# A hybrid decoder layer on one core: the second pair of x tiles is loaded behind the modulation weights

## The chip, the core and the metric

The kernel runs on one core of one Trainium2 chip. Its engines are TensorE (PE, with PEld for the loading of its stationary operand), VectorE (DVE), ScalarE (ACT), GpSimd (POOL) and SyncE (SP). SP and POOL issue the DMA transfers of this kernel, each from a queue of its own: q1 is that of SP, q0 that of POOL. The metric is the time of one execution on the device, in microseconds (us), as the median of several.

## What is computed

One decoder layer with two kinds of heads side by side. Only its beginning matters here:

```python
shift, scale, gate = split(c @ w_ada + b_ada, 3)     # c: (1, 1024), w_ada: (1024, 3072)
h = rms_norm(x, norm_g) * (1 + scale) + shift        # x: (2048, 1024)
u = h @ w_in                                         # all inputs of the heads, gates among them
# mLSTM heads and forgetting attention on u, then
x = x + gate * (concat(heads) @ w_out)
```

So nothing can be projected before `shift` and `scale` are known, and they need two thirds of `w_ada` (8 MB) and the whole of `c`.

## The kernel before

The sequence has 2048 tokens, in four blocks `b` of 512; the model width of 1024 is cut into eight slices `k` of 128. All engines run instruction streams of their own that are written out by hand and meet at semaphores; there is no scheduler. What follows is the first stage (`modulate_and_project`), up to about 98 us of the profile.

**Loads.** x comes in pairs of tiles of 128 tokens, 1 MB each, into a ring of four buffers: pairs 0 and 1 in `u_copy`, pair 2 in `work`, pair 3 in `stage[:, 1]`. `load_x(i)` (L246) issues one. The modulation weights come in five pieces (`PIECES`, `load_piece`, L242) of 2, 2, 2, 1 and 1 rows of 128 x 2048 numbers, a MB each row, into `ada_rows`. SP issues in this order: c, pair 0, pair 1, the five pieces, pair 2, a weight tile of `w_in`, pair 3, the gates' columns, another weight tile (L252 to L262). Pairs 4 to 7 are issued as the ring comes free, pairs 4 and 5 when the eight slices of block 0 have been transposed (L265). Beside it POOL issues 13 small parameter loads (L334 to L347), which all count up `param_landed`.

**Modulation.** PE transposes c and the parameters (L754, L756; the second waits for all 13 loads). DVE copies both out, and then adds up the eight rows of `w_ada`, each times its column of c, into `ada_sum` (L478, L481), each as its piece lands. 16 products of one column (L810, counted as 32 in the trace) sum that over the partitions into `ps_mod`, and three short DVE instructions make `scale`, `shift` and `gain` (L488 to L492), of which `mod_ready` tells.

**x.** For each pair i ACT takes squares and a root (`root_mean_square(i)`, L869 and L872), DVE takes the reciprocal (`inverse(i)`, L449), and ACT multiplies the two tiles by it (`scale_x(i)`, L893); for pairs 4 to 7 DVE does the multiplication (`normalize`, L456).

**The steps.** There are 32 steps, at = 8 b + k. In each, PE transposes slice k of the four tiles of block b into PSUM (`turn_x`, L771, four transposes), ACT modulates it (`modulate`, L880), and DVE splits the result in a high and a low part (`split_h`, L464 and L466). PE then multiplies them with the first weight tile and the gates' columns (`first_products`, L783, three products; `gate_products`, L797, two). The products of a step stand in PE's stream behind the turn of four steps later (`LAG`). For block 0 there is room in PSUM for five turns (`ps_first`), and they are issued first of all, ahead of L810. `turn_x(b, 0)` waits until all four tiles of its block are scaled; `turn_x` of b > 0 also until ACT has taken the slice two steps before; `modulate` also until DVE has split the slice two steps before.

After the stage the projections of the other tiles follow on PE (L703), which need every block of h, and everything later stands behind them.

Of the kernel before, what the change touches and what calls it, by code (L numbers as in the profile page):

```python
# [71 lines left out]
def modulate_and_project(nc, block, a, scratch, keep, fox):  # L72

    with ExitStack() as ctx:
# [19 lines left out]
        with ExitStack() as late:  # L94
# [142 lines left out]
            def _(sp):  # L237
# [15 lines left out]
                load_x(0)  # L253
                load_x(1)
                for q in range(len(PIECES)):
                    load_piece(q)
                load_x(2)
                load_w(0, F_Q)
# [170 lines left out]
            def _(dve):  # L429
# [41 lines left out]
                inverse(0)  # L471
                inverse(1)
                dve.wait_ge(c_ready, 1)
                for q, (first, end) in enumerate(PIECES):
                    dve.wait_ge(piece_landed[q], 16)
                    for k in range(first, end):
                        if k == 0:
                            dve.tensor_scalar(ada_sum, ada_rows[k], c_cols[:, k:k + 1], None, ALU.mult).then_inc(ada_added, 1)  # L478
                        else:
                            dve.wait_ge(ada_added, k)  # L480
                            dve.scalar_tensor_tensor(out=ada_sum, in0=ada_rows[k], scalar=c_cols[:, k:k + 1], in1=ada_sum,  # L481
                                                     op0=ALU.mult, op1=ALU.add).then_inc(ada_added, 1)
                split_w(0, 1, 0)
                dve.wait_ge(half_free, 1)
                inverse(2)
                inverse(3)
                dve.wait_ge(mod_psum, 1)
# [5 lines left out]
                                         in1=params[:, ADA_ROWS + 2 * KT:ADA_ROWS + 3 * KT],  # L493
                                         op0=ALU.add, op1=ALU.mult).then_inc(mod_ready, 1)

                def split_gates():
# [11 lines left out]
                for b in range(TB):  # L508
                    for k in range(KT):
                        split_h(b, k)  # L510
                        if (b, k) == (0, 0):
                            split_gates()
                        if 0 < b < TB - 1 and k in (2, 5):
                            normalize((b + 1) * G_PAIRS + (k == 5))
                    if b == 1:
                        split_w(1, 1, 1)
# [173 lines left out]
            def _(pe):  # L690
# [112 lines left out]
                ahead = len(ps_first)  # L803
                for k in range(ahead):
                    turn_x(0, k)
                pe.wait_ge(zeroed, 5)
                pe.wait_ge(ada_added, KT)
                for col in range(2 * KT):
                    first = (D_MODEL + col * P) % (2 * D_MODEL)
                    ins = pe.matmul(ps_mod[:, col:col + 1], ada_sum[:, first:first + P], one[:, :], start=True, stop=True)  # L810
                ins.then_inc(mod_psum, 1)
                done = 0
                for at in range(ahead, TB * KT + LAG):
# [39 lines left out]
            def _(act):  # L853
# [40 lines left out]

                for i in range(ON_ACT * G_PAIRS):
                    root_mean_square(i)
                    if i == 1:
                        scale_x(0)
                        scale_x(1)
                scale_x(2)  # L900
                act.wait_ge(mod_ready, 3)
                for b in range(TB):
                    for k in range(KT):
                        modulate(b, k)
                        if b == 0 and k in (1, 3):
                            scale_x(3, [k // 2])
                        if 0 < b < TB - 1 and k in (1, 4):
                            root_mean_square((b + 1) * G_PAIRS + (k == 4))
                        if b and k == 5:
                            take_gates(b - 1)  # L910
# [1276 lines left out]
```

## Time and profile before

| | us |
|---|---|
| median of 3 runs | 1593.19 |
| lowest and highest | 1592.62, 1593.48 |
| span of the profiled execution | 1588.24 |
| start of the first product of a step (L783) in it | 43.72 |
| start of the turn that opens block 1 (L771) | 50.52 |
| start of the squares of pair 4 (L869) | 54.33 |
| start of the projections behind the stage (L703) | 97.94 |

The span counts from the first to the last recorded work of the core. The profiled execution's time by the clock of the runs is not recorded; the span is 4.95 us less than the median, and this is taken as what lies around it. In the profile's page the chain of waits is followed back from the last instruction: at each step to what released it. PE is busy for 95% of the span.

### The profile page before, as it was taken

The page shows a single profiled execution, that of the slowest core. Times are in us where ns is not written, and L with a number is a line of the kernel's source. Part 1 is how long each engine was busy: PE and PEld are TensorE (multiplying, and loading weights), DVE is VectorE, ACT ScalarE, POOL GpSimd, SP SyncE. Part 2 cuts the span into 40 slices and gives each one's busy share as a digit, 9 for nine tenths or more (in the row PEclk, how much of TensorE's full clock was granted, in tenths as well). Part 3 has the DMA queues.
Part 4 walks back from the last instruction along what each step waited for, and adds up shares of the span by engine and source line. Part 5 has one row for each costly group of instructions (what it writes and reads, how often), then busy time and mean ns, then how long its engine had stood idle before and what let it go on. Part 6 is the DMA issues. An engine that isn't in the chain of part 4 may idle for free.

```text
span 1588.2 us, 21410 instructions
## 1 busy us (share of the span) xinstructions
PE 1515.7 (95%) x7913; PEld 1152.1 (73%) x7913; DVE 792.8 (50%) x1835; ACT 533.7 (34%) x812; POOL 174.9 (11%) x237
## 2 busy tenths in 40 slices
PE   2999999999899999999999899999999997999998
PEld 2677877887788888888888665555555555888886
DVE  5845445321120100355541585766766747677674
ACT  4842323201111111222211566565655644222220
POOL 2000000002000000000000312103112000222121
PEclk8999999999999999999999999999999998999999
DMA  9313133241341311121232534223161037576761
GB/s 346 133 32 131 68 132 112 101 145 34 107 149 61 99 67 65 42 79 53 79 132 80 151 102 133 54 75 126 45 177 46 16 91 241 175 189 184 182 198 54
DMA packets 128569, 178.09 MB, mean 112 GB/s; under 512 B 8764, under 2 KB 90824, under 8 KB 123416
## 3 DMA queue, kind: packets, MB, share of 16 engines
q1 hardware_dynamic: 119488, 129.75, 27.5%
q0 software_dynamic: 9008, 47.36, 7.9%
q8 instruction: 46, 0.75, 0.2%
q14 instruction: 27, 0.22, 0.1%
HBM read 116.93 MB, written 60.16 MB: 112 GB/s over the span
## 4 chain that ended last, share of the span: by engine, by line
PE 80%; DVE 8%; ACT 5%; DMA 3%; issue 2%; POOL 1%; SPq 0%; DVEq 0%; POOLq 0%; ACTq 0%
PE a_ps_u L703 26%; PE a_ps_u L745 14%; PE m_ps_out L1804 11%; PE f_ps_o L1341 8%; PE f_ps_t L1316 7%; PE f_ps_s L1304 7%; PE a_ps_u L727 1%; DVE stage L481 1%; DVE u_copy L547 1%; DVE stage L555 1%; ACT work L928 1%; PE m_ps_m L1779 1%; ACT work L930 1%; PE m_ps_m L1780 1%; PE m_ps_m L1783 1%
## 5 line engine op out<-in xcount | busy, mean ns | idle before, releaser
L703 PE MATMUL a_ps_u<-a_h_hi,w_in_hi 128*128 128x512 f32 x736 | 286.9, 390 | 0.9 <-DVEq L519 0.9
L703 PE MATMUL a_ps_u<-a_h_lo,w_in_hi 128*128 128x512 f32 x736 | 286.6, 389 | 0.0
L703 PE MATMUL a_ps_u<-a_h_hi,w_in_lo 128*128 128x512 f32 x736 | 198.1, 389 | 0.0
L703 PEld LDWEIGHTS a_ps_u<-a_h_hi,w_in_hi 128*128 128x128 f32 x736 | 138.1, 188 | 31.8 <-issue 3.2
L703 PEld LDWEIGHTS a_ps_u<-a_h_hi,w_in_lo 128*128 128x128 f32 x736 | 138.2, 188 | 28.8
L703 PEld LDWEIGHTS a_ps_u<-a_h_lo,w_in_hi 128*128 128x128 f32 x736 | 138.2, 188 | 28.2
L745 PE MATMUL a_ps_u<-v_hi,a_h_hi 128*128 128x512 f32 x384 | 150.5, 392 | 6.4 <-ACT stage L957 6.4
L745 PE MATMUL a_ps_u<-v_hi,a_h_lo 128*128 128x512 f32 x384 | 150.3, 392 | 0.0
L437 DVE CAST w_in_hi<-w_in_land 128x1024 fp32r<-128x1024 f32 x24 | 16.6, 691 | 178.4 <-PE a_ps_u L703 93.5
L1474 ACT ACTIVATE f_probs_t<-f_ps_t 128x512 f32<-128x512 f32 (+1 forms) x128 | 65.2, 548 | 98.4 <-PE f_ps_t L1316 98.4
L957 ACT ACTIVATE stage<-a_ps_u 128x512 f32<-128x512 f32 x48 | 28.3, 597 | 198.8 <-PE a_ps_u L745 196.8
L745 PEld LDWEIGHTS a_ps_u<-v_hi,a_h_hi 128*128 128x128 f32 x384 | 72.7, 189 | 22.1 <-ACT stage L957 6.8
L1804 PE MATMUL m_ps_out<-m_w_hi,w_in_hi 128*128 128x512 f32 x256 | 86.4, 414 | 2.0 <-DVE m_update L1957 2.0
L745 PEld LDWEIGHTS a_ps_u<-v_hi,a_h_lo 128*128 128x128 f32 x384 | 72.6, 189 | 15.0
L1341 PE MATMUL f_ps_o<-f_probs_t,v_tok 128*64 128x512 f32 (+1 forms) x320 | 79.9, 577 | 2.5 <-DVE f_probs_t L1403 1.4
L1804 PE MATMUL m_ps_out<-m_w_lo,w_in_hi 128*128 128x512 f32 x256 | 82.1, 397 | 0.0
L1804 PE MATMUL m_ps_out<-m_w_hi,w_in_lo 128*128 128x512 f32 x256 | 81.2, 394 | 0.0
L362 POOL DMA_DIRECT2D scratch_arrays<-stage x29 | 18.3, 630 | 529.8 <-ACTq L960 219.6
L745 PE MATMUL a_ps_u<-v_lo,a_h_hi 128*128 128x512 f32 x192 | 75.6, 394 | 0.0
L1341 PE MATMUL f_ps_o<-work,v_tok 128*64 128x512 f32 (+2 forms) x320 | 73.1, 536 | 1.2 <-DVE work L1403 1.2
L1403 DVE COPY work<-f_ps_t 128x512 f32<-128x512 f32 (+1 forms) x80 | 46.5, 582 | 48.5 <-PE f_ps_t L1316 48.3
L576 DVE CAST v_hi<-w_in_land 128x512 fp32r<-128x512 f32 x24 | 10.2, 426 | 120.6 <-PE a_ps_u L745 119.5
(291 smaller groups left out, 2695.8 us busy)
## 6 DMA issues: line engine op xcount, KB each, us to landing
scratch_arrays<-stage POOLq DMA_DIRECT2D x27, 1024.0 KB, 4.6
scratch_qkT<-stage POOLq DMA_DIRECT2D x8, 2048.0 KB, 7.7
w_in_land<-in_w_in SPq DMA_DIRECT2D x24, 512.0 KB, 7.2
w_in_land<-scratch_arrays SPq DMA_DIRECT2D x32, 256.0 KB, 4.8
m_x_in<-in_x SPq DMA_DIRECT2D x16, 512.0 KB, 4.6
out<-m_result SPq DMA_DIRECT2D x15, 512.0 KB, 3.0
a_ada_rows<-in_w_ada SPq DMA_DIRECT2D x3, 2048.0 KB, 16.5
w_in_land<-in_w_in SPq DMA_DIRECT2D x24, 256.0 KB, 3.3
```

Of the source, the lines that this page charges most:

```text
L362: pool.dma_start(out, sb_view).then_inc(stored, 16)
L437: dve.tensor_copy(w_hi[:, par], w_land[:, par]).then_inc(hi_ready, 1)
L481: dve.scalar_tensor_tensor(out=ada_sum, in0=ada_rows[k], scalar=c_cols[:, k:k + 1], in1=ada_sum, op0=ALU.mult, op1=ALU.add).then_inc(ada_a ...
L703: ins = pe.matmul(ps_u[:, par, b, :], w[:, k, :], h[:, k, cols], start=(k == 0 and i < 2 * len(blocks) and h is h_hi), stop=(k == KT - 1 a ...
L745: ins = pe.matmul(ps_u[:, half, c, :], h[:, k, first:first + P], w, start=(k == 0 and h is h_hi and w is not v_lo[k]), stop=(k == KT - 1 a ...
L957: act.activation(view[:, :, c, :], ps_u[:, u % 2, c, :].rearrange("p (j f) -> p j f", f=P), func).then_inc(v_taken, 1)
L1304: ins = pe.matmul(banks[h][:, 0:width], q_in[J][own, q, rows], k_in[c][own, k, 0:width], start=(q == HI and k == HI), stop=(k == LO))
L1316: ins = pe.transpose(ps_t[:, u % T_BANKS, r * P:(r + 1) * P], probs(n, J, h, r, slice(kt * P, (kt + 1) * P)), ident[:, :])
L1341: ins = pe.matmul(ps_o[h * F_DH:(h + 1) * F_DH, first:], v_tok[:, kt, h, :], probs_t[s % 2][:, h, first:], start=(kt == 0), stop=(kt == ke ...
L1403: dve.tensor_copy(probs_t[s % 2][:, h, first:], ps_t[:, u % T_BANKS, first:]).then_inc(taken_by_dve, 1)
L1474: act.activation(probs_t[s % 2][:, h, first:], ps_t[:, u % T_BANKS, first:], ACT.Copy).then_inc(copied_by_act, 1)
L1804: ins = pe.matmul(ps_out[:, b, :], part[:, par, k, :], w[:, k, b * NB:(b + 1) * NB], start=(k == 0 and part is y_hi and w is w_hi), stop=( ...
```

## The change

SP issues pair 1 behind the five pieces of weights. ACT works through pair 0 wholly and then through pair 1; it takes the squares of pair 2, scales pair 2 only between the first modulations, and takes the squares of pair 3 behind the modulation of slice 3. DVE's reciprocals move accordingly: that of pair 1 behind the eight sums, that of pair 2 behind `gain`, that of pair 3 behind the split of slice 4. PE's first five turns move behind the products of L810.

```diff
@@ SP
                 load_x(0)
-                load_x(1)
                 for q in range(len(PIECES)):
                     load_piece(q)
+                load_x(1)
                 load_x(2)
@@ DVE
                 inverse(0)
-                inverse(1)
                 dve.wait_ge(c_ready, 1)
                 for q, (first, end) in enumerate(PIECES):
...
+                inverse(1)
                 split_w(0, 1, 0)
                 dve.wait_ge(half_free, 1)
-                inverse(2)
-                inverse(3)
                 dve.wait_ge(mod_psum, 1)
...
                                          op0=ALU.add, op1=ALU.mult).then_inc(mod_ready, 1)
+
+                inverse(2)
...
                         split_h(b, k)
                         if (b, k) == (0, 0):
                             split_gates()
+                        if (b, k) == (0, 4):
+                            inverse(3)
@@ PE
                 ahead = len(ps_first)
-                for k in range(ahead):
-                    turn_x(0, k)
                 pe.wait_ge(zeroed, 5)
                 pe.wait_ge(ada_added, KT)
...
                 ins.then_inc(mod_psum, 1)
+                for k in range(ahead):
+                    turn_x(0, k)
                 done = 0
@@ ACT
-                for i in range(ON_ACT * G_PAIRS):
+                for i in range(2):
                     root_mean_square(i)
-                    if i == 1:
-                        scale_x(0)
-                        scale_x(1)
-                scale_x(2)
+                    scale_x(i)
+                root_mean_square(2)
                 act.wait_ge(mod_ready, 3)
                 for b in range(TB):
                     for k in range(KT):
                         modulate(b, k)
-                        if b == 0 and k in (1, 3):
-                            scale_x(3, [k // 2])
+                        if b == 0 and k in (1, 2):
+                            scale_x(2, [k - 1])
+                        if b == 0 and k == 3:
+                            root_mean_square(3)
+                        if b == 0 and k in (5, 6):
+                            scale_x(3, [k - 5])
```

PE's stream before, from the parameters' transpose (70 columns) to the first product. `stage` is `ada_sum` here, `u_copy` are pairs 0 and 1:

```order
L756 MATMUL a1_ps_u<-ident,modulated 128x70 [waits param_landed]
L771 MATMUL a1_ps_u<-ident,u_copy 128x128 [waits a_x_scaled_act,a_half_free]
L771 MATMUL a1_ps_u<-ident,u_copy 128x128 x19
L810 MATMUL a1_ps_u<-a1_one,stage 128x1 [waits a_ada_added,a_zeroed]
L810 MATMUL a1_ps_u<-a1_one,stage 128x1 x15
L771 MATMUL a1_ps_u<-ident,u_copy 128x128 [waits a_modulated_ready]
L771 MATMUL a1_ps_u<-ident,u_copy 128x128 x3
L783 MATMUL a1_ps_u<-a_h_hi,w_in_hi 128x512 [waits a_w_split,a_split_done]
```

The same stretch of PE in the changed kernel, whose lines are numbered a little higher:

```order
L758 MATMUL a1_ps_u<-ident,modulated 128x70 [waits param_landed]
L810 MATMUL a1_ps_u<-a1_one,stage 128x1 [waits a_ada_added,a_zeroed,a_half_free]
L810 MATMUL a1_ps_u<-a1_one,stage 128x1 x15
L773 MATMUL a1_ps_u<-ident,u_copy 128x128 [waits a_x_scaled_act]
L773 MATMUL a1_ps_u<-ident,u_copy 128x128 x19
L773 MATMUL a1_ps_u<-ident,u_copy 128x128 [waits a_modulated_ready]
L773 MATMUL a1_ps_u<-ident,u_copy 128x128 x3
L785 MATMUL a1_ps_u<-a_h_hi,w_in_hi 128x512 [waits a_w_split,a_split_done]
```

The 20 transposes have moved from ahead of the one-column products to behind them; what follows is unchanged.

ACT's stream before, from the squares of pair 3 (in `stage`) to the squares of pair 4 (in `u_copy`); `work` is pair 2:

```order
L869 ACTIVATE squares,a1_sumsq<-stage 128x1024 [waits a_ring_landed3]
L869 ACTIVATE a_h_hi,a1_sumsq<-stage 128x2x512
L872 ACTIVATE a1_rms<-a1_sumsq,eps 128x2 [waits a_sumsq_ready]
L893 ACTIVATE work<-work,a1_rstd 128x1024 [waits a_rstd_ready]
L893 ACTIVATE work<-work,a1_rstd 128x1024
L880 ACTIVATE modulated<-a1_ps_u,a1_shift,a1_gain 128x512 [waits a_xt_psum,a_mod_ready]
L880 ACTIVATE modulated<-a1_ps_u,a1_shift,a1_gain 128x512 [waits a_xt_psum]
L893 ACTIVATE stage<-stage,a1_rstd 128x1024 [waits a_rstd_ready]
L880 ACTIVATE modulated<-a1_ps_u,a1_shift,a1_gain 128x512 [waits a_split_done,a_xt_psum] x2
L893 ACTIVATE stage<-stage,a1_rstd 128x1024 [waits a_rstd_ready]
L880 ACTIVATE modulated<-a1_ps_u,a1_shift,a1_gain 128x512 [waits a_split_done,a_xt_psum] x6
L869 ACTIVATE squares,a1_sumsq<-u_copy 128x1024 [waits a_ring_landed0]
```

ACT's stream in the changed kernel, from the first modulation to the squares of pair 4:

```order
L882 ACTIVATE modulated<-a1_ps_u,a1_shift,a1_gain 128x512 [waits a_xt_psum]
L895 ACTIVATE work<-work,a1_rstd 128x1024 [waits a_rstd_ready]
L882 ACTIVATE modulated<-a1_ps_u,a1_shift,a1_gain 128x512 [waits a_split_done,a_xt_psum]
L895 ACTIVATE work<-work,a1_rstd 128x1024 [waits a_rstd_ready]
L882 ACTIVATE modulated<-a1_ps_u,a1_shift,a1_gain 128x512 [waits a_split_done,a_xt_psum]
L871 ACTIVATE squares,a1_sumsq<-stage 128x1024 [waits a_ring_landed3]
L871 ACTIVATE a_h_hi,a1_sumsq<-stage 128x2x512
L874 ACTIVATE a1_rms<-a1_sumsq,eps 128x2 [waits a_sumsq_ready]
L882 ACTIVATE modulated<-a1_ps_u,a1_shift,a1_gain 128x512 [waits a_split_done,a_xt_psum] x2
L895 ACTIVATE stage<-stage,a1_rstd 128x1024 [waits a_rstd_ready]
L882 ACTIVATE modulated<-a1_ps_u,a1_shift,a1_gain 128x512 [waits a_split_done,a_xt_psum]
L895 ACTIVATE stage<-stage,a1_rstd 128x1024 [waits a_rstd_ready]
```

Two scalings of pair 2 and the squares and root of pair 3, which stood ahead of the first modulation, stand among the first seven of them now; the scalings of pair 3 have moved back behind slices 5 and 6.

## Rows read from the trace of the kernel before

**Rows 1.** The page: span, and busy time, share and instructions of each engine.

```profile
span 1588.2 us, 21410 instructions
PE 1515.7 (95%) x7913; PEld 1152.1 (73%) x7913; DVE 792.8 (50%) x1835; ACT 533.7 (34%) x812; POOL 174.9 (11%) x237
```

**Rows 2.** The chain that ended last, 0 to 120 us: start, length, what.

```profile
8.28 6.82 DMA a_gate_bias<-in_b_fgate_f
...
15.92 1.20 DVE stage L478
...
31.73 2.37 DVE stage L481
34.23 6.97 PE a_ps_u L810 x32
41.70 0.79 ACT modulated L880
...
49.31 4.99 DMA u_copy<-in_x
54.33 1.15 ACT squares L869 x2
...
56.75 0.77 ACT modulated L880
```

**Rows 3.** DMA issues of pieces 1, 2, 5: tile, queue, KB, us to landing.

```profile
a_ada_rows<-in_w_ada SPq DMA_DIRECT2D x1, 2048.0 KB, 12.1
a_ada_rows<-in_w_ada SPq DMA_DIRECT2D x1, 2048.0 KB, 16.5
a_ada_rows<-in_w_ada SPq DMA_DIRECT2D x1, 1024.0 KB, 24.7
```

**Rows 4.** DMA queues at 7:8.5, then 8.7:12: packets, MB, share of the engines.

```profile
q1 hardware_dynamic: 143, 0.59, 97.6%
q0 software_dynamic: 109, 0.02, 6.7%
...
q1 hardware_dynamic: 163, 1.33, 98.9%
q0 software_dynamic: 164, 0.01, 3.6%
```

**Rows 5.** Timeline of ACT, 39 to 53 us: start, length, instruction, idle time before.

```profile
41.70 1.45 ACT L880 ACTIVATE modulated<-a_ps_u,a_shift,a_gain 128x512 f32<-128x512 f32 x2 [0.41 <-DVE a_gain L492]
43.05 1.14 ACT L893 ACTIVATE stage<-stage,a_rstd 128x1024 f32<-128x1024 f32 x1
44.08 0.77 ACT L880 ACTIVATE modulated<-a_ps_u,a_shift,a_gain 128x512 f32<-128x512 f32 x1
```

**Rows 6.** Timeline of PE, 20 to 52.3 us.

```profile
20.31 4.50 PE L771 MATMUL a_ps_u<-ident,u_copy 128*128 128x128 f32 x20 [4.79 <-ACT u_copy L893]
...
42.54 1.12 PE L771 MATMUL a_ps_u<-ident,u_copy 128*128 128x128 f32 x4 [1.34 <-ACT modulated L880]
43.72 0.80 PE L783 MATMUL a_ps_u<-a_h_hi,w_in_hi 128*128 128x512 f32 x1
...
45.92 0.39 PE L783 MATMUL a_ps_u<-a_h_hi,w_in_hi 128*128 128x512 f32 x1
...
47.07 0.60 PE L771 MATMUL a_ps_u<-ident,u_copy 128*128 128x128 f32 x4
...
50.52 0.41 PE L771 MATMUL a_ps_u<-ident,work 128*128 128x128 f32 x2
...
52.14 0.38 PE L771 MATMUL a_ps_u<-ident,work 128*128 128x128 f32 x2
```

**Rows 7.** Stretches: length, PE busy (instructions), clock, DMA share, GB/s.

```profile
28.80:32.00 3.20, 0.00 (x0) 0.50 1.04 379
...
1569.45:1571.50 2.05, 0.01 (x1) 1.00 0.00 0
1571.60:1574.90 3.30, 3.30 (x8) 0.50 0.08 32
```

## Prediction

> **What bounds the kernel now.** I read the page first, then the chain of waits, then the timelines of single engines in the stretch that the change touches. PE is busy for 95% of a span of 1588.2 us [rows 1], and from the projections at 97.94 us on the chain runs on PE with little beside it, so whatever moves that start moves the end. The question is therefore what sets the time of the first stage.
>
> The chain [rows 2] tells it in four pieces. First, the last of POOL's 13 small parameter loads: issued at 8.28, landed 6.82 us later, at 15.10; PE transposes the parameters and DVE copies them. Second, DVE's sum over the eight rows of w_ada: it starts at 15.92 and then runs without a gap, one row of 1.20 and seven of 2.37, to 34.10. Third, the one-column products: 34.23 to 41.20. Fourth, the first modulation at 41.70. From there the chain goes through the steps: at 49.31 the load of pair 4 is released, takes 4.99 us, its squares start on ACT at 54.33, and the next modulation, of slice 2 of block 1, at 56.75. The reader is to see two things. The sum over w_ada is paced by DVE and not by the loads, although closely: the first two pieces, issued at 2.3 and 2.9, need 12.1 and 16.5 us and so land at 14.4 and 19.4, and DVE takes row 2 (the first of piece 2) at 19.60; the last piece, issued at 4.6, lands at 29.3 and is taken at 31.73 [rows 2, 3]. And before the first modulation ACT had nothing left to do but to wait 0.41 us for it [rows 5]: the squares of pairs 2 and 3 and the scaling of pair 2 lie beside L810.
>
> **Part 1, the load that moves.** Pair 1 (1 MB) leaves the place ahead of the pieces, so each piece lands about 2.5 us earlier (piece 2, of 2 MB, took from 14.4 to 19.4 [rows 3]). That is worth nothing by itself: DVE starts its sum when the parameters are copied, at 15.9 us, and then never waits for a piece. Pair 1 lands where the last piece landed, at about 29, its squares (2.4 us) are done at 31.6, its reciprocal follows the sum on DVE and costs the products of L810 nothing, and ACT scales it in 2.2 us, by about 36.6 us, ahead of the end of L810 at 41.2. The second reciprocal ahead of the sum goes away, which is under 0.1 us. Pairs 2 and 3 land as before, since the bytes ahead of them are the same.
>
> **Part 2, the parameters.** What the start of the sum hangs on is POOL's queue, and the two queues share the 16 DMA engines. Between 8.7 and 12 us, in 3.3 us, they moved 163 packets of SP's queue and 164 of POOL's: one each in turn, though POOL's packets are tiny (0.01 MB in all). The 163 were 1.33 MB, so 8 KB each, rows of w_ada. In the 1.5 us from 7 to 8.5, while x was loading with packets of 4 KB (143 for 0.59 MB), 109 packets of POOL's got through [rows 4]. So beside x POOL got 73 packets a us, and can get SP's 95 once its loads are all under way; beside w_ada it gets 50. The change takes the packets of 4 KB of pair 1 away and puts those of 8 KB there. For some 1.1 us, up to 8.6, POOL then gets 45 a us less, 50 packets in all, and at 50 a us they take 1.0 us at the end: the parameters land at 16.1 and not at 15.1. The bounds are 0.3 us (109 packets against 75 in the 1.5 us of the row, half of it made up for while POOL still issues) and 1.6 us (the loss of 45 a us for all of the 1.8 us in which both run beside x). I take 1.0. With it DVE's sum, L810 and all behind them start 1.0 later.
>
> The Trainium skill (DMA: Bandwidth & Descriptors, the part on one DMA of the GpSimd path) gives such a load about 2.0 us plus bytes over 436 GB/s. By that the last parameter would land at 10.3, and the sum would start when the first piece lands: at 14.4 before, at about 11.9 after, and this part would be a gain of 2.5 us and not a loss of 1.0, the time 1595.2. The trace has 6.82 us for a load of a few bytes, so the row decides.
>
> **Part 3, the five turns.** They took 4.50 us for 20 transposes at 20.3 us, hidden under DVE's sum [rows 6]. Behind L810 nothing hides them. The clock is at its half level there (granted 0.50 from 28.8 on [rows 7]; the products are at their full pace from 45.9 on [rows 6]), and one turn of four costs 0.90 of PE and is ready 1.12 us after its start [rows 6]. Without Part 2: the first turn starts at 41.1 and is done at 42.2, and ACT's first modulation starts at 42.25 and not at 41.70; the second waits for its turn until 43.15.
>
> **Part 4, ACT's order.** The turn that opens block 1 waits for both scalings of pair 3. Their price, start to start: a modulation 0.68 (41.70, two, then 43.05), a scaling 1.03 (43.05 to 44.08), squares and root of a pair 2.42 (54.33 to 56.75) [rows 2, 5]. Before, two scalings lay between the first modulations; now it is four, and squares. ACT goes: slice 0 at 42.25, slice 1 at 43.15, scaling 43.83, slice 2 44.87, scaling 45.55, slice 3 46.59, squares and root of pair 3 47.27, slice 4 49.69, slice 5 50.37. The scaling of pair 3 then needs the reciprocal, and that is queued on DVE behind the split of slice 4: modulation 49.69, plus 0.81 until DVE starts, plus the split of 1.16, plus 0.2: 51.9. Scaling 51.9, slice 6 52.9, scaling 53.6, done 54.8. The turn that opens block 1 starts at 54.85, where it started at 50.52 [rows 6]. Behind it on PE stand the products of slice 4 and all later ones, which have long been ready; PE waits some 3 us. The next turn follows 1.62 later (50.52 to 52.14 [rows 6]), at 56.47, its modulation at 57.1, and the squares of pair 4 start on ACT at 57.8, where they started at 54.33: 3.4 us later. Pair 4 is no longer waited for: its load is released by the last turn of block 0, at about 50.6, and lands at 55.6. From the squares of pair 4 on the order is as before, and the chain went through ACT and DVE there, so nothing takes the 3.4 us back.
>
> **Part 5, the clock.** PE now waits some 3.2 us before the turn that opens block 1. In this trace the granted clock fell after each wait of PE of 2.05 us or more behind the start: at 1571.5 after one of 2.05 us, to the half level for the 3.3 us that followed [rows 7]. There are five such waits, and it stayed up in the two of 1.4 us. So I expect it to fall. At the half level a turn costs 0.9 instead of 0.4 and the products of a step 2.2 (43.72 to 45.92) instead of 1.15 (45.92 to 47.07) [rows 6]; for some 3.4 us PE does half its work, at most 1.7 us lost, and there PE has nothing to spare. The bounds are 0 (no fall, or one that comes late) and 1.7. I take 1.1.
>
> **Sum.** 3.4 (turns and ACT's order) + 1.0 (parameters) + 1.1 (clock) = 5.5 us. Made on the profiled span, 1588.2 goes to 1593.7; with the 4.95 us around it, 1593.19 + 5.5 = 1598.7 us.
>
> **Rivals.** (a) The clock stays up: 3.4 + 1.0, 1597.6. For it: the wait may be cut by an earlier or later rise than at 45.8. Against it: all five waits above 2 us.
> (b) The parameters land as before: 3.4 + 1.1, 1597.7, or 1596.6 without the fall of the clock. For it: POOL issues until 8.8 us whatever the engines do.
> (c) Not slower: POOL's loads stand behind the bytes of SP's queue, not behind its packets, and with pair 1 gone they land up to 2.5 us earlier, at 12.6, and the sum starts at 13.4. Then 3.4 - 2.5 = +0.9, 1594.1, and 1595.2 with the clock's fall. With that fall it brings the change within 0.2% from a landing at 13.8 or earlier. Against it: one packet in turn with one, in rows 4.
> (d) Faster: the pieces pace the sum after all, by 2.5 us, and ACT's later order is hidden by the wait for pair 4: +0.5 for the first turn, 1593.19 - 2.5 + 0.5 = 1591.2. Against it: the sum has no gap, and ACT alone needs 13.3 us from slice 0 to the squares of pair 4 (ten modulations 6.8, four scalings 4.1, squares 2.4), where 12.6 lay between them before.
> The Trainium skill (TensorE: Matmul & The Clock Gate, on transposes) says that transposes do not count as work for the clock. The 20 transposes of this trace were followed by a granted clock of 1.00 until 28.7, which does not bear it out; by the rule the clock would rise only after the first products, PE would wait less, and the result would be (a).
>
> **How the numbers follow.** The forecast has 0.50, (a) 0.15, (b) 0.13, (c) 0.12, (d) 0.06, and 0.04 is for more than 1600.3 (a clock that stays down longer). The range leaves out (c), (d) and that last: 1595.8 to 1600.3; its ends are +2.6 (the walk of Parts 3 and 4 short by 0.8, nothing for parameters and clock) and +7.1 (3.8 for the walk, 1.6, 1.7). 0.2% is 3.2 us, about what a measurement can tell from no change. (b) without the clock lies just at it, and 0.04 of its chance go to no change. Slower by more: 0.78; within: 0.16; faster: 0.06.
>
> **What would show it.** The parameters' last landing at 16.1 (15.1 denies Part 2, 12.6 is (c)). L810 at 35.2 and as long as before. 20 transposes behind it in 4.5 us. The reciprocal of pair 3 behind slice 4, a wait of PE of about 3 us ahead of the turn that opens block 1, at 55.9. The granted clock at 0.50 behind it. Squares of pair 4 at 58.8 to 59.9, L703 at 103.4. Wrong would be the prediction above all if a wait for pair 4 or a slack behind block 1 takes the delay back, so that L703 starts less than 3 us later.

## The result and the profile after

| | before | changed |
|---|---|---|
| median | 1595.35 us of 9 runs (1592.62 to 1595.97) | 1598.49 us of 9 runs (1597.36 to 1600.99) |
| ratio | 1 | 1.0024, 95% interval 1.0014 to 1.0034 |
| span of the profiled execution | 1588.24 | 1596.5 |
| parameters transposed (L756, L758 after) | 15.14 | 15.98 |
| one-column products start (L810) | 34.23 | 35.01 |
| first modulation | 41.70 | 43.02 |
| turn that opens block 1 | 50.52 | 55.27 |
| squares of pair 4 | 54.33 | 58.24 |
| turn that opens block 2 | 65.41 | 69.32 |
| projections start (L703, L705 after) | 97.94 | 102.04 |

The change makes the kernel slower by 0.24%, 3.8 us of 1595 (2.2 to 5.4 by the interval). The medians themselves are 3.1 us apart. The stage ends 4.1 us later in the profiled execution. Forecast were 5.5 us.

The span differs by 8.3 us, twice that. The other half arises behind the stage: what the profiled executions of the 14 kernels here need from the start of the projections to the end scatters from 1487.2 to 1496.9 us (1490.3 before, 1494.5 changed), with no reordering there. The granted clock falls at other places in each, many of them between 1290 and 1360 us; that this makes the scatter is not shown (over 1290 to 1345 us the granted clock is 0.91 in both kernels). The profiled execution of before was a short one: the profiled run of the changed kernel took 2.06 us more than its span, and by the same difference that of before took about 1590.3 us, and not 1593.19. Where the time went is therefore read up to L703, stage by stage, and the medians are the check.

PE's timeline of the changed kernel, 7 to 130 us (start, length, instruction, idle time before and what ended it), to be held against [rows 2] and [rows 6]:

```profile
15.98 0.38 PE L758 MATMUL a_ps_u<-ident,modulated 70*128 70x70 f32 x1 [13.21 <-DMA a_gate_bias<-in_b_fgate_f]
...
35.01 6.96 PE L810 MATMUL a_ps_u<-a_one,stage 128*128 128x1 f32 x32 [18.65 <-DVE stage L480]
41.82 5.36 PE L773 MATMUL a_ps_u<-ident,u_copy 128*128 128x128 f32 x24
46.84 0.78 PE L785 MATMUL a_ps_u<-a_h_hi,w_in_hi 128*128 128x512 f32 x1
...
55.27 0.44 PE L773 MATMUL a_ps_u<-ident,work 128*128 128x128 f32 x2 [2.19 <-ACT stage L895]
...
69.32 0.66 PE L773 MATMUL a_ps_u<-ident,u_copy 128*128 128x128 f32 x4 [0.91 <-DVE u_copy L456]
```

The parameters come 0.84 us later. The turns, 24 transposes with the sixth, follow the one-column products at once, and PE has no gap there. Ahead of the turn that opens block 1, where it did not wait before, it now idles for 2.19 us, for ACT's scaling of pair 3.

ACT's timeline of the changed kernel, 29 to 66 us, beside [rows 5]:

```profile
43.02 1.57 ACT L882 ACTIVATE modulated<-a_ps_u,a_shift,a_gain 128x512 f32<-128x512 f32 x2 [3.46 <-PE a_ps_u L773]
44.49 1.14 ACT L895 ACTIVATE work<-work,a_rstd 128x1024 f32<-128x1024 f32 x1
...
47.89 1.06 ACT L871 ACTIVATE squares<-stage 128x1024 fp32r<-128x1024 f32 x1
...
52.37 1.15 ACT L895 ACTIVATE stage<-stage,a_rstd 128x1024 f32<-128x1024 f32 x1 [0.63 <-DVE a_rstd L449]
53.42 0.76 ACT L882 ACTIVATE modulated<-a_ps_u,a_shift,a_gain 128x512 f32<-128x512 f32 x1
54.09 1.14 ACT L895 ACTIVATE stage<-stage,a_rstd 128x1024 f32<-128x1024 f32 x1
...
58.24 1.05 ACT L871 ACTIVATE squares<-u_copy 128x1024 fp32r<-128x1024 f32 x1
```

ACT idles 3.46 us ahead of the first modulation (0.41 before), and then works through two scalings and a pair's squares that lay ahead of it before. The 0.63 us are the reciprocal of pair 3, queued on DVE behind the split of slice 4. The squares of pair 4 wait for nothing: ACT comes to them last.

The DMA queues of the changed kernel at 7 to 8.5 us and at 8.7 to 12, beside [rows 4]:

```profile
q1 hardware_dynamic: 74, 0.61, 95.3%
q0 software_dynamic: 66, 0.02, 5.4%
...
q1 hardware_dynamic: 174, 1.29, 96.5%
q0 software_dynamic: 174, 0.01, 3.5%
```

In the first stretch SP's packets are now 8 KB (0.61 MB in 74), and POOL gets 66 through where it got 109.

### The profile page after: what moved, and what is told of

Same layout as the page of the kernel before. It is cut to its first block and busy times, and to the rows that moved or that the text cites. A ratio compares the mean times of both kernels' runs of the same rounds, so it can differ in the third digit from the quotient of the medians.

```text
span 1596.5 us, 21409 instructions
## 1 busy us (share of the span) xinstructions
PE 1513.8 (95%) x7913; PEld 1151.2 (72%) x7913; DVE 791.9 (50%) x1835; ACT 533.4 (33%) x812; POOL 175.4 (11%) x237
## 5 line engine op out<-in xcount | busy, mean ns | idle before, releaser
L705 PE MATMUL a_ps_u<-a_h_hi,w_in_hi 128*128 128x512 f32 x736 | 287.0, 390 | 0.9 <-DVEq L521 0.9
L705 PE MATMUL a_ps_u<-a_h_lo,w_in_hi 128*128 128x512 f32 x736 | 286.6, 389 | 0.0
L705 PE MATMUL a_ps_u<-a_h_hi,w_in_lo 128*128 128x512 f32 x736 | 198.0, 389 | 0.0
L705 PEld LDWEIGHTS a_ps_u<-a_h_hi,w_in_hi 128*128 128x128 f32 x736 | 138.1, 188 | 31.7 <-issue 3.2
L705 PEld LDWEIGHTS a_ps_u<-a_h_hi,w_in_lo 128*128 128x128 f32 x736 | 138.1, 188 | 28.8
L705 PEld LDWEIGHTS a_ps_u<-a_h_lo,w_in_hi 128*128 128x128 f32 x736 | 138.2, 188 | 28.2
L1478 ACT ACTIVATE f_probs_t<-f_ps_t 128x512 f32<-128x512 f32 (+1 forms) x128 | 65.1, 548 | 101.2 <-PE f_ps_t L1320 101.2
```

What stands on the lines that cost most here:

```text
L705: ins = pe.matmul(ps_u[:, par, b, :], w[:, k, :], h[:, k, cols], start=(k == 0 and i < 2 * len(blocks) and h is h_hi), stop=(k == KT - 1 a ...
L1478: act.activation(probs_t[s % 2][:, h, first:], ps_t[:, u % T_BANKS, first:], ACT.Copy).then_inc(copied_by_act, 1)
```

## The experiments

The theory to be tested (P for its part on packets, A for its part on ACT) has four terms: the parameters land later because SP's packets beside them are larger; the turns cost 0.5 to 1.3 us; ACT's order costs most; the granted clock falls if PE waits long. Its rivals were that the place of the load, or the turns alone, cost the time, and that the landing of the parameters is scatter. The columns up to L703 are the steps of the table above, in us from the start of the profiled execution: "opens 1" and "opens 2" are the turns that open blocks 1 and 2. The ratios are against the kernel before on the same chip, whose median was 1594.67 us beside the kernels from load_back to small_early and 1593.62 beside the last four. The intervals reach 1.6 to 2.1 us to either side, so terms of about 1 us are read from the profiles.

| kernel | params | L810 | first mod. | opens 1 | squares 4 | opens 2 | L703 | median | ratio (95%) |
|---|---|---|---|---|---|---|---|---|---|
| before | 15.14 | 34.23 | 41.70 | 50.52 | 54.33 | 65.41 | 97.94 | 1595.35 | 1 |
| changed | 15.98 | 35.01 | 43.02 | 55.27 | 58.24 | 69.32 | 102.04 | 1598.49 | 1.0024 (1.0014 to 1.0034) |
| load_back | 15.17 | 34.21 | 42.22 | 54.48 | 58.97 | 70.05 | 102.62 | 1598.31 | 1.0023 (1.0011 to 1.0035) |
| early_squares | 15.83 | 34.87 | 42.88 | 52.72 | 57.98 | 69.07 | 101.67 | 1595.74 | 1.0005 (0.9992 to 1.0018) |
| turns_late | 15.26 | 34.36 | 42.37 | 51.19 | 55.19 | 66.27 | 98.84 | 1594.54 | 1.0003 (0.9992 to 1.0015) |
| act_late | 15.32 | 34.42 | 41.96 | 54.14 | 58.96 | 70.44 | 103.31 | 1596.52 | 1.0013 (0.9999 to 1.0026) |
| small_packets | 13.42 | 32.45 | 40.47 | 52.72 | 56.49 | 68.01 | 100.85 | 1593.68 | 0.9997 (0.9984 to 1.0009) |
| small_back | 13.66 | 34.60 | 42.61 | 54.87 | 58.97 | 70.15 | 102.88 | 1596.32 | 1.0013 (1.0 to 1.0025) |
| before_small | 13.46 | 34.55 | 42.01 | 51.62 | 56.91 | 68.00 | 100.57 | 1592.83 | 0.9996 (0.9983 to 1.001) |
| small_early | 13.69 | 32.73 | 40.74 | 50.58 | 55.61 | 66.70 | 99.28 | 1592.16 | 0.9985 (0.9972 to 0.9999) |
| late_params | 15.70 | 31.44 | 39.48 | 51.74 | 56.29 | 67.37 | 99.93 | 1593.52 | 1.0001 (0.999 to 1.0011) |
| all_four | 15.75 | 31.58 | 39.62 | 49.46 | 52.43 | 63.51 | 96.07 | 1590.08 | 0.9977 (0.9965 to 0.9989) |
| all_four_back | 15.15 | 34.12 | 42.15 | 52.00 | 54.97 | 66.04 | 98.55 | 1592.49 | 0.9998 (0.9987 to 1.0009) |
| before_turns_first | 15.10 | 34.27 | 41.74 | 51.70 | 54.61 | 65.69 | 98.20 | 1592.33 | 0.9991 (0.9979 to 1.0002) |

The columns and the ratios agree only roughly. In all 13 kernels L703 is later against before than the ratio says, by 0.3 us (changed) to 3.7 us (small_early): small_packets starts L703 2.9 us later than before and is no slower. The stage of the one profiled execution of before may have been a short one; no second one shows it. Differences between the other kernels do not hang on it.

**The load alone undone: load_back.**

```diff
 load_x(0)
+load_x(1)
 for q in range(len(PIECES)):
     load_piece(q)
-load_x(1)
```

> The changed kernel with pair 1 loaded ahead of the pieces again; every engine's order stays as changed. Theory P (packets): beside pair 1's packets of 4 KB the parameter loads get through faster again, so the parameters' transpose is at 15.1 us as before and not at 15.98, and everything behind it is 0.8 us earlier than in the changed kernel: the turn that opens block 2 at 68.5 (69.32 changed, 65.41 before), +3.1 us against before in all. Rival Q (the parameters' landing is scatter of one execution and has nothing to do with pair 1): transpose at 15.5 to 16.2, turn at 69.3, +3.9 us. Rival L (it was the load's place that cost the time, since pair 1 came late): the turn at 66 or earlier, +0.5 us at most.

The parameters are back at 15.17, the products of L810 0.80 us earlier, as is every step up to the turn that opens block 1 (54.48 for 55.27): theory P, and not the place of the load. The other kernels bear it out: where SP's rows are of 8 KB, the parameters are transposed at 15.10 to 15.32 in the six kernels with pair 1 ahead of the pieces and at 15.70 to 15.98 in the four with it behind. Behind that turn the execution loses 1.5 us more. PE's stretches of load_back (length, busy, granted clock) show by what:

```profile
51.20:54.30 3.10, 0.00 (x0) 1.00 0.89 351
54.50:57.70 3.20, 3.20 (x10) 0.50 0.71 284
58.00:60.00 2.00, 2.00 (x14) 1.00 0.00 0
```

PE waited 3.56 us, and the granted clock was at the half level for the 3.2 us behind it. From the turn that opens block 1 to the squares of pair 4 it took 4.49 us (54.48 to 58.97), in the changed kernel 2.97 (55.27 to 58.24), so the fall costs 1.5 us here.

**ACT's order and the turns, one at a time, in the kernel before: act_late and turns_late.**

```diff
 # act_late: ACT (DVE's reciprocals of pairs 2 and 3 accordingly)
-                for i in range(ON_ACT * G_PAIRS):
+                for i in range(3):
...
-                scale_x(2)
...
+                        if b == 0 and k in (1, 2):
+                            scale_x(2, [k - 1])
+                        if b == 0 and k == 3:
+                            root_mean_square(3)
+                        if b == 0 and k in (5, 6):
+                            scale_x(3, [k - 5])
 # turns_late: PE, the first five turns
-                for k in range(ahead):
-                    turn_x(0, k)
...
                 ins.then_inc(mod_psum, 1)
+                for k in range(ahead):
+                    turn_x(0, k)
```

> The kernel before with the changed order of ACT and DVE for pairs 2 and 3 (scalings of pair 2 behind slices 1 and 2, squares of pair 3 behind slice 3, its scalings behind slices 5 and 6, reciprocals accordingly), loads and PE as before. Theory A: first modulation at 41.70, the turn that opens block 1 at 54.0 to 54.3 (50.52 before) with PE waiting 2 to 3.8 us for it, the turn that opens block 2 at 68.0 to 69.0 (65.41 before), +2.6 to +3.5 us, nearly the whole of the 3.1 that is not the parameters'. Rival F: under +1 us. Rival C (the granted clock falls in PE's wait): a stretch at 0.50 behind the turn and 1 to 1.7 us more.

> The kernel before with PE's first five turns behind the one-column products, nothing else. Theory A: the first modulation waits for its turn, 42.25 and not 41.70, and the fifth turn and so the release of pair 4 come about 1.3 us later; the turn that opens block 2 at 66.0 to 66.8 (65.41 before), +0.6 to +1.4 us. Rival F (the turns are the main cost): the turn at 68 or later, +2.7 us or more.

ACT's order alone moves the turn that opens block 1 from 50.52 to 54.14, 3.6 us. The one that opens block 2 is 5.0 us late, since here too PE waited (3.41 us) and the clock fell. From the one turn to the other act_late needs 16.30 us and the changed kernel, in the same order of ACT and without a fall, 14.05; with 14.05 it would be 2.8 us late. (Before needs 14.89, with 0.76 us of waiting for pair 4 in it.) The turns alone cost 0.67 us at the first modulation (0.54 beyond this execution's later parameters) and 0.86 at the turn that opens block 2. Theory A, and rival F falls.

**ACT's gap filled in the changed kernel: early_squares.**

```diff
                 root_mean_square(2)
+                root_mean_square(3)
                 act.wait_ge(mod_ready, 3)
...
-                        if b == 0 and k == 3:
-                            root_mean_square(3)
```

> The changed kernel with the squares and the root of pair 3 ahead of the first modulation, where ACT waited 3.46 us, and the reciprocal of pair 3 behind that of pair 2; nothing else. Theory A (ACT's order sets the turn that opens block 1): 2.4 us of ACT and the 0.6 us wait for the reciprocal leave the stretch, the turn that opens block 1 comes 2 us earlier (53.2, not 55.27), PE hardly waits, and the squares of pair 4 are then bound by the landing of pair 4, 5.0 us behind the last turn of block 0, at 56.9 and not 58.24; the turn that opens block 2 at about 67.6 (69.32 changed), +2.2 us against before. Rival F (the five turns behind the one-column products cost the time, ACT's order is hidden): no change against the changed kernel, turn at 69.3, +3.9 us.

The turn that opens block 1 comes at 52.72, 2.55 us earlier, and PE does not wait for it. But only 0.25 us of that reaches the turn that opens block 2. ACT's timeline:

```profile
55.02 0.78 ACT L881 ACTIVATE modulated<-a_ps_u,a_shift,a_gain 128x512 f32<-128x512 f32 x1 [0.82 <-PE a_ps_u L772]
57.98 1.06 ACT L870 ACTIVATE squares<-u_copy 128x1024 fp32r<-128x1024 f32 x1 [2.19 <-DMA u_copy<-in_x]
```

Released at 51.55 and 6.4 us under way (5.0 in the kernels before and changed), pair 4 lands after ACT is free. I had expected its landing to bind, at 56.9; it cost 1.1 us more. The ratio is better than this stage: 1.0005 against 1.0024, about 3 us, of which L703 shows 0.4; where the rest comes from is open. ACT's order and the release of pair 4 are two bounds close to each other, and the second shows when the first goes.

**The parameters' landing by the size of SP's packets: small_packets, small_back, before_small.**

```diff
-sp.dma_start(ada_land[:, first:end, :], ada_view[:, first:end, 0:2 * D_MODEL]).then_inc(piece_landed[q], 16)
+for half in range(2):
+    cols = slice(half * D_MODEL, (half + 1) * D_MODEL)
+    sp.dma_start(ada_land[:, first:end, cols], ada_view[:, first:end, cols]).then_inc(piece_landed[q], 16)
```

> The changed kernel with each piece of weights loaded in two halves of 1024 columns, so that SP's packets are 4 KB and not 8 KB there; the same bytes in the same order. Theory P (POOL's packets go one in turn with SP's, so the size of SP's packets sets when the parameters land): they land near 13 us, the sum over w_ada starts then and is now paced by the pieces, the last of which lands near 26.8; sum ends at 29.3 to 30.5 (34.9 changed), first modulation 37.3 to 38.5 (43.02 changed), turn that opens block 2 at 63.6 to 65 (69.32 changed, 65.41 before): 4 to 6 us less than the changed kernel. Rival Q (the parameters' landing has nothing to do with packets): parameters' transpose at 15.9, everything as in the changed kernel, within 0.5 us. Rival B (small packets are slower): pieces land later, and the time is longer.

> The same with pair 1 loaded ahead of the pieces again. Theory P: the parameters land near 13 us here too, the sum is paced by the pieces, which land 2.5 us later than in small_packets, so the sum ends at about 31.8 and the turn that opens block 2 comes 1.5 to 2.5 us later than in small_packets, still 3 us ahead of the changed kernel: the moved load is worth 2 us once the parameters are out of the way. Rival L (the place of pair 1 makes no difference): both within 0.5 us.

> The kernel before with the pieces in halves as in small_packets. Theory P: parameters near 13 us, sum ended at 31.8 (34.1 before), one-column products until 38.8; but ACT has the squares of pair 3 (landing at 36.7) and the scaling of pair 2 ahead of its first modulation, which so starts at 41.4 and not 41.70: turn that opens block 2 at 65.1 (65.41 before), 0.3 us less. Rival: 2.4 us less, if the first modulation follows the products at once.

The same bytes in packets of 4 KB bring the parameters at 13.4 to 13.7 in all three kernels, 2.3 to 2.6 us earlier than in the changed one. The queues of small_packets between 8.7 and 12 us:

```profile
q1 hardware_dynamic: 331, 1.28, 97.4%
q0 software_dynamic: 245, 0.02, 5.1%
```

The same 1.3 MB of SP's, and POOL gets 245 packets through for 174. With load_back this shows Part 2's mechanism twice. The packets no longer go one for one (245 of POOL's for SP's 331), and the landing is not at 13.0; what holds it there was not tested.

The sum starts at 14.06 in small_packets, and 2.6 us of gain arrive at the first modulation, less than expected, as DVE paces the sum from there on. In small_back and before_small the early parameters gain nothing. DVE's timeline of before_small:

```profile
14.60 1.28 DVE L480 TENSOR_SCALAR stage<-a_ada_rows,a_c_cols 128x2048 f32<-128x2048 f32 x1 [0.36 <-DMA a_ada_rows<-in_w_ada]
15.92 2.35 DVE L483 SCALAR_TENSOR_TENSOR stage<-a_ada_rows,a_c_cols,stage 128x2048 f32<-128x2048 f32 x1
19.64 4.74 DVE L483 SCALAR_TENSOR_TENSOR stage<-a_ada_rows,a_c_cols,stage 128x2048 f32<-128x2048 f32 x2 [1.37 <-DMA a_ada_rows<-in_w_ada]
24.75 9.65 DVE L483 SCALAR_TENSOR_TENSOR stage<-a_ada_rows,a_c_cols,stage 128x2048 f32<-128x2048 f32 x4 [0.37 <-DMA a_ada_rows<-in_w_ada]
```

It takes row 2 at 19.64, where the kernel before took it at 19.60: now it waits there for the second piece. So my expectation that the sum would end at 31.8 was wrong, and with it that small_back would be 3 us ahead of the changed kernel: it opens block 2 at 70.15, 0.8 us behind it. In the kernel before two things held the sum, the parameters and the second piece, and they came within 0.2 us of each other [rows 2, 3]; either alone earlier gains nothing. The moved load takes the one away and leaves the other. With both away it pays: small_packets against small_back, which differ in the place of pair 1 alone, 2.0 to 2.5 us at every step from L810 on, and 2.6 us in the medians.

before_small missed by more than that at the turn that opens block 2: 68.00, where I had expected 65.1 and the kernel before has 65.41. Pair 4 was released at 50.66 (49.31 before) and was 6.24 us under way (4.99), so that ACT waited 2.28 us for it. The products of block 0 took 0.63 us each until 48.0, in the kernel before until 45.6, and the late release goes with that; why the transfer took longer is not shown.

**small_early** is small_packets with the edit of early_squares.

> small_packets with the squares of pair 3 ahead of the first modulation (as in early_squares). Theory A: pair 3 lands at 36.7, its squares end at 39.2, first modulation 39.2 (2 us later than in small_packets), the turn that opens block 1 at 49 without a long wait of PE, squares of pair 4 when it has landed, 5 to 6.5 us behind the last turn of block 0, near 54; turn that opens block 2 at 64 to 65.5, about as small_packets. Rival: 2 us better than small_packets, as 2.4 us of ACT leave the stretch between the first modulation and the turn that opens block 1.

The turn that opens block 2 is at 66.70, 1.3 us earlier than in small_packets, in which the clock fell; squares of pair 4 waited 1.95 us for the landing. I had expected the first modulation 2 us later than in small_packets; it was 0.3 us later (40.74), since it came at 40.47 and not at 37.3 in small_packets, and by then the squares of pair 3 are done in small_early (ACT waits 1.00 us behind them).

**The parameters out of the sum's way without other packets: late_params.** DVE's copy of the parameters moves behind the sum, which does not need them.

```diff
-                dve.wait_ge(param_psum, 1)
-                dve.tensor_copy(params[:, :], ps_h[1][:, 0:PARAM_ROWS]).then_inc(half_free, 1)
                 inverse(0)
...
+                dve.wait_ge(param_psum, 1)
+                dve.tensor_copy(params[:, :], ps_h[1][:, 0:PARAM_ROWS]).then_inc(half_free, 1)
                 inverse(1)
```

> The changed kernel with DVE's copy of the parameters moved from ahead of the sum over w_ada to behind it (only scale, shift and gain need them). Theory P (the parameters' landing holds the start of the sum, and with pair 1 moved nothing else does): the sum starts when the first piece lands, at 12 us and not 16.6, and is then paced by the pieces: the third lands near 21.8 and four sums of 2.4 follow, so it ends at 31.4 and not 34.9; one-column products at 31.6, first modulation near 39.6 (43.02 changed), the turn that opens block 2 at 65.9 to 67.5 (69.32 changed): 3.4 us less than changed, where the granted clock does not differ. Rival Q (the pieces pace the sum in the changed kernel already): within 0.5 us.

The parameters still land late (15.70), but the sum starts at 11.87, when the first piece lands, and L810 at 31.44: 3.57 us earlier than changed. The turn that opens block 2 gains 1.95 of it in this execution, in which PE waited 3.54 us and the clock fell (0.69 us for that turn's first half, 0.44 in the changed kernel).

**Everything that the moved load needs: all_four and all_four_back.** all_four joins late_params and early_squares, and moves PE's last three turns of block 0 ahead of the first products, which releases pair 4 earlier:

```diff
                 for k in range(ahead):
                     turn_x(0, k)
+                for k in range(ahead, KT):
+                    turn_x(0, k)
                 done = 0
+                while done < LAG:
+                    first_products(done)
+                    gate_products(done)
+                    done += 1
-                for at in range(ahead, TB * KT + LAG):
+                for at in range(KT, TB * KT + LAG):
```

> late_params, and the squares of pair 3 ahead of the first modulation (early_squares), and the last three turns of block 0 ahead of the first products, so that pair 4 is released some 5 us earlier. Theory: first modulation 39.5, the turn that opens block 1 near 49.5, squares of pair 4 at 52.4 to 53.2 without a wait for its landing (57.98 in early_squares, 2.19 us of it waiting), the turn that opens block 2 at 63.5 to 64.3 (65.41 before, 69.32 changed): 1 to 2 us less than before, 5 to 6 less than changed. Rival (the landing of pair 4 is not what held early_squares, but ACT is): 65.5 or later.

> all_four with pair 1 loaded ahead of the pieces again: the worth of the moved load when nothing else holds the sum. Theory P: the pieces land 2.5 us later, the sum ends at 33.9 and not 31.4, the turn that opens block 2 2 to 2.5 us later than in all_four, about as before. Rival L (the place of pair 1 is worth nothing): within 0.5 us of all_four.

all_four beats both kernels: 0.9977 (0.9965 to 0.9989) of before, 3.7 us less, with the stage ended 1.9 us earlier than before and 6.0 earlier than changed. ACT's timeline of all_four, in which no step waits for pair 4:

```profile
51.76 0.78 ACT L887 ACTIVATE modulated<-a_ps_u,a_shift,a_gain 128x512 f32<-128x512 f32 x1 [0.82 <-PE a_ps_u L772]
52.43 1.05 ACT L876 ACTIVATE squares<-u_copy 128x1024 fp32r<-128x1024 f32 x1
```

With pair 1 ahead of the pieces again all steps come 2.5 us later (and the median 2.4 us), and nothing is left of the gain (0.9998): L810 starts at 34.12, as before, although the sum does not wait for the parameters there, since the pieces hold it. So the moved load is worth 2.5 us, once the sum does not wait for the parameters and ACT and pair 4 do not take it back.

**before_turns_first** is the edit to PE alone, in the kernel before.

> The kernel before with the last three turns of block 0 ahead of the first products, nothing else. Theory (squares of pair 4 waited 0.76 us for its landing): squares of pair 4 at 53.5 to 53.7, turn that opens block 2 at 64.6 (65.41 before), 0.8 us less. Rival: the first products, which start 1.2 us later, hold the steps behind them, and nothing is gained or up to 1 us lost.

The wait for pair 4 is gone, but the products start later and the turn that opens block 1 with them (51.70 for 50.52): squares at 54.61. The rival holds; the ratio of 0.9991 (0.9979 to 1.0002) tells it from no change in neither direction.

## Why the prediction was right, point by point

**Bound.** Right that DVE's sum, behind the parameters, set the first modulation, and that a start of L703 moves the end. Only half right that the pieces did not matter: the second came 0.2 us ahead of need, so the pieces were a second bound at the same place, and the forecast used that only for (c) and (d).

**Part 1, the load.** Worth nothing by itself, as forecast: DVE never waits for a piece in the changed kernel, and its sum only starts later. Pair 1's squares began at 29.48 (29 forecast), its scaling ended at 37.16 (36.6, plus 0.8 for the later sum).

**Part 2, the parameters.** 1.0 forecast, 0.78 measured at the start of L810; the mechanism is confirmed by load_back and the packets of 4 KB. From 7 to 8.5 us 43 packets of POOL's fewer got through (66 for 109), which at the 50 a us of [rows 4] are 0.86 us; 50 packets were forecast. Rivals (b) and (c) fall.

**Part 3, the turns.** Forecast +0.55 at the first modulation; measured 43.02 - 41.70 - 0.78 = 0.54.

**Part 4, ACT's order.** Parts 3 and 4 together 3.4 forecast at the squares of pair 4; measured 58.24 - 54.33 - 0.78 = 3.13. The turn that opens block 1 was forecast for 54.85 without Part 2; 55.27 - 0.78 = 54.5. act_late confirms that this is ACT's. (The walk ends at 57.8, which is 3.5 and not 3.4 behind 54.33.)

**Part 5, the clock.** This is the term that was mis-sized: 1.1 forecast, 0 in the profiled execution. What was wrong in it first is the length of PE's wait. I had PE's products at full pace from 45.8 on, as before; here they are from 48 on only, so PE came to the end of block 0 later and waited 2.19 us, not 3.2. First PE's timeline of the changed kernel, then its stretches, as in [rows 7]:

```profile
47.41 0.61 PE L785 MATMUL a_ps_u<-a_h_lo,w_in_hi 128*128 128x512 f32 x1
47.84 0.42 PE L785 MATMUL a_ps_u<-a_h_hi,w_in_lo 128*128 128x512 f32 x1
48.09 0.40 PE L799 MATMUL a_ps_u<-a_h_hi,a_w_gates 128*88 128x512 f32 x1
```

```profile
53.40:55.20 1.80, 0.00 (x0) 1.00 0.83 314
55.30:57.70 2.40, 2.40 (x15) 1.00 1.03 423
```

```profile
51.74 0.69 PE L773 MATMUL a_ps_u<-ident,work 128*128 128x128 f32 x2 [3.54 <-ACT stage L895]
...
53.08 0.63 PE L785 MATMUL a_ps_u<-a_h_lo,w_in_hi 128*128 128x512 f32 x1
...
56.12 0.39 PE L799 MATMUL a_ps_u<-a_h_hi,a_w_gates 128*88 128x512 f32 x1
```

In the eight kernels with early squares or with ACT as before, PE waits 1.1 us or less ahead of that turn, and it did not fall there. So the fall comes with this order of ACT. From the turn that opens block 1 to the one that opens block 2 the five need 15.28 to 16.30 us, the changed kernel 14.05: a fall costs 1.2 to 2.3 us. The changed kernel's profiled execution had the shortest of the six waits and no fall; that the shortness spared it is not shown, and how many of its nine runs have a fall can't be told from their times.

The premise was weaker than it looked. All five waits above 2 us in the trace of before were followed by a fall, but of the 12 traces in which PE waits 2.68 or 2.69 us ahead of four transposes late in the kernel (L1769 before), seven show a fall within 1 us behind it and five none. PE's timelines of before and of all_four:

```profile
1326.38 1.11 PE L1769 MATMUL m_ps_y<-ident,w_in_land 128*128 128x128 f32 x4 [2.68 <-DVE m_scores L1892]
...
1323.34 0.66 PE L1777 MATMUL m_ps_y<-ident,w_in_land 128*128 128x128 f32 x4 [2.68 <-DVE m_scores L1900]
```

The wait is the same, and the four transposes behind it run at the half level (1.11 us) or at the full one (0.66).

**Sum.** 3.13 + 0.78 = 3.91 at the turn that opens block 2 and 4.10 at L703, against 4.4 forecast without the clock: rival (a) rather than the likeliest case. That the time of 1598.7 us was met to 0.2 us (1598.49) is luck: the difference was forecast at 5.5 us and measured at 3.8, and the median of before came out 2.16 us higher with nine runs (1595.35) than with the three that the forecast started from (1593.19). The 4.95 us around the span were misread: 2.06 lie there, and the rest is that the profiled execution was shorter than the median. That did not enter the difference.

When the clock comes up is not set by PE's stream alone: in the changed kernel the full pace came behind the first products, and in load_back, with the same stream of PE, the first product already had it (0.47 us), as in all_four.

Rival (d) falls: no piece held the sum, and the squares of pair 4 waited for nothing. Its second half, that the wait for pair 4 hides ACT's order, is what early_squares showed from the other side: there the wait hides most of what the earlier squares gain.

## What to carry to other kernels

A transfer that is issued earlier helps only what waits for it last: look for the second thing that arrives at the same time, here tiny parameters on another queue, and move what waits for both. Beside a stream in rows of 8 KB the small transfers here got one packet for one of the stream's, and the same bytes in rows of 4 KB brought them 2.3 to 2.6 us earlier, so the size of the stream's rows is a thing to try. And work that hides in an engine's wait ahead of a stage costs its full length once it is moved into the stage.

## What the runs showed of the hardware

- A load of a few bytes on POOL's queue took 6.8 us beside rows of 4 and then 8 KB, 7.6 us beside rows of 8 KB alone, and 5.1 us beside rows of 4 KB; 163 packets of one queue passed for 164 of the other.
- Transposes bring the granted clock up, though not each time. In the kernel before PE did nothing from 15.5 to 34.2 us but 20 transposes, at 20.31 and for 4.50 us (the half pace), and the granted clock fell to 0.50 at 28.7, so it had risen. before_small has the same 20, at 18.63 and for 4.50 us, and no fall is recorded behind them; its products still took 0.63 us at 45. In load_back PE ran only the one-column products and then 24 transposes from 41.02; these took 4.32 us, in the changed kernel 5.36:

```profile
41.02 4.32 PE L773 MATMUL a_ps_u<-ident,u_copy 128*128 128x128 f32 x24
45.10 0.47 PE L785 MATMUL a_ps_u<-a_h_hi,w_in_hi 128*128 128x512 f32 x1
```

  The first product behind them has the full pace (0.47 us; 0.78 in the changed kernel). That speaks against what the Trainium skill says in TensorE: Matmul & The Clock Gate on PE-mode transpose, that transposes do not count as busy for the clock. The 7 us of one-column products ahead of them left it at half: in three kernels (before, act_late, before_turns_first) the granted clock is 0.50 all through them, and in no kernel did the transposes behind them start at the full pace (in load_back 10 took 0.80 us from 44.2 on, but all 24 took 4.32, and in no kernel did 24 take less).
- No length of PE's wait alone decides whether the granted clock falls. Waits of 2.05 us (1571.5 in the kernel before) and of 2.96 to 3.56 us were followed by the half level, one of 2.19 us was not, nor one of 2.91 us (1299.3 in small_early); one of 2.68 us was in seven traces and not in five. In the changed kernel it fell at 1324.5, 1.6 us behind a wait of 1.36 us.
